# Even layer of a two-block network: a new order of slabs, and latent attention and token shift placed beside other work

## The reference

```python
u = rmsnorm_2(h, norm_mix)
proj = u @ w_in                                   # 1024 x 2208
rw_cols, mla_cols = proj[..., :1792], proj[..., 1792:]
rw_prev = jnp.pad(rw_cols[:, :-1], ((0, 0), (1, 0), (0, 0)))
rw_cols = rw_cols + shift_mu * (rw_prev - rw_cols)          # token shift
y_a = rwkv7_time_mix(...)    # delta rule, 8 heads of 64, group norm, bonus, gate
y_b = mla_attention(...)     # latent attention: norms, q, k, v, rotary, causal softmax, 8 heads
h = h + jnp.concatenate([y_a, y_b], axis=-1) @ w_out
return h + swiglu(rmsnorm_2(h, norm_ffn), ffn_wg, ffn_wu, ffn_wd)
```

## Time and profile before

| | us |
|---|---|
| median of 3 runs (lowest, highest) | 3005.59 (3005.14, 3008.46) |
| the profiled execution's own time | 3002.98 |
| its span, first to last instruction | 3001.2 |
| TensorE, weight loads, VectorE, ScalarE busy | 2737.8, 2273.0, 1806.4, 1453.1 |
| mean granted TensorE clock | 0.941 |
| first split product of the even layer | 1199.8 |
| first transpose of the delta rule | 1301.6 |
| output projection begins, ends | 1555.8, 1583.8 |

### The profile page before, as it was taken

One profiled execution on the slowest core, in us unless ns is written; L12 is line 12 of the kernel. 1 busy time (PEld: TensorE's weight loads), 2 busy tenths in 40 slices (PEclk: granted clock), 3 DMA queues, 4 the chain that ended last, 5 costly groups with the idle time before them and its releaser, 6 DMA issues.

```text
span 3001.2 us, 38726 instructions
## 1 busy us (share of the span) xinstructions
PE 2737.8 (91%) x15370; PEld 2273.0 (76%) x15370; DVE 1806.4 (60%) x1887; ACT 1453.1 (48%) x1609; POOL 29.5 (1%) x40
## 2 busy tenths in 40 slices
PE   6999889999788998857679999889999999999998
PEld 3875368888676898847559997678888888888886
DVE  3224455543544785352344553488888888888887
ACT  3225133332334554311134443367777777777775
POOL 0001000000001000000000000000000000000000
PEclk8999999999898999977689999989999999999999
DMA  7546322222231445300014453179999999999996
GB/s 296 189 188 253 112 84 85 98 96 87 79 146 62 151 160 182 118 1 1 1 52 148 168 181 141 43 279 362 343 346 361 348 361 347 343 362 348 360 347 234
DMA packets 84359, 589.81 MB, mean 197 GB/s; under 512 B 9872, under 2 KB 10000, under 8 KB 19472
## 3 DMA queue, kind: packets, MB, share of 16 engines
q1 hardware_dynamic: 82800, 576.16, 51.7%
q10 hardware_dynamic: 1440, 11.93, 1.0%
HBM read 587.01 MB, written 1.05 MB: 196 GB/s over the span
## 4 chain that ended last, share of the span: by engine, by line
PE 85%; DVE 9%; ACT 4%; issue 1%; DMA 1%; POOL 0%; ACTq 0%; DVEq 0%; SPq 0%; POOLq 0%
PE banks L453 22%; PE banks L454 21%; PE banks L455 21%; PE banks L459 19%; DVE ring_rounded L515 1%; ACT ring_rounded L505 1%; DMA ring<-in_stream 1%; PE banks L2530 1%; DVE rstd L729 1%; ACT scratch L869 1%; DVE activations L1289 1%; PE banks L805 0%; DVE nmax L841 0%; DVE aT L742 0%; DVE aT L1947 0%
## 5 line engine op out<-in xcount | busy, mean ns | idle before, releaser
L515 DVE TENSOR_TENSOR ring_rounded<-ring,ring_rounded 128x2048 fp32r<-128x2048 f32 (+3 forms) x162 | 328.0, 2028 | 460.8 <-ACT ring_rounded L505 459.9
L454 PE MATMUL banks<-ring_rounded,activations_rounded 128*128 128x512 f32 x1344 | 527.5, 392 | 0.0
L454 PE MATMUL banks<-aT_rounded,ring_rounded 128*128 128x256 f32 (+1 forms) x1552 | 501.4, 323 | 0.0
L505 ACT ACTIVATE ring_rounded<-ring 128x2048 fp32r<-128x2048 f32 (+3 forms) x162 | 274.9, 1701 | 396.5 <-PE banks L455 381.1
L453 PE MATMUL banks<-aT_rounded,ring_rounded 128*128 128x256 f32 (+1 forms) x1104 | 332.7, 301 | 20.4 <-DVE aT_rounded L751 11.6
L455 PE MATMUL banks<-aT_rounded,ring_rounded 128*128 128x256 f32 (+1 forms) x1104 | 330.9, 300 | 0.0
L454 PEld LDWEIGHTS banks<-aT_rounded,ring_rounded 128*128 128x128 f32 x1552 | 301.9, 194 | 21.0
L454 PEld LDWEIGHTS banks<-ring_rounded,activations_rounded 128*128 128x128 f32 x1344 | 252.7, 188 | 52.3
L2704 DVE TENSOR_TENSOR ring_rounded<-ring,tables_rounded 128x2048 fp32r<-128x2048 f32 x112 | 253.7, 2287 | 23.3 <-ACT tables_rounded L2622 22.6
L2704 DVE TENSOR_TENSOR ring_rounded<-ring,aT_rounded 128x2048 fp32r<-128x2048 f32 x112 | 254.4, 2286 | 11.6 <-ACT aT_rounded L2622 11.0
L2622 ACT ACTIVATE tables_rounded<-ring 128x2048 fp32r<-128x2048 f32 x112 | 215.0, 1920 | 89.7 <-DMA ring<-in_stream 76.4
(11 more groups left out here) (302 smaller groups left out, 4899.6 us busy)
## 6 DMA issues: line engine op xcount, KB each, us to landing
ring<-in_stream SPq DMA_DIRECT2D x501, 1024.0 KB, 5.4
ring<-in_stream SPq DMA_DIRECT2D x32, 704.0 KB, 5.5
ring<-in_stream SPq DMA_DIRECT2D x28, 768.0 KB, 6.2
activations<-in_rpb ACTq DMA_DIRECT2D x2, 1536.0 KB, 6.5
ring<-in_stream SPq DMA_DIRECT2D x6, 512.0 KB, 5.0
tables<-in_tab_b ACTq DMA_DIRECT2D x1, 2436.0 KB, 8.6
tables<-in_tab_a ACTq DMA_DIRECT2D x1, 2304.0 KB, 8.9
hT<-in_h ACTq DMA_DIRECT2D x1, 2048.0 KB, 15.5
```

Source lines behind the costliest of these rows:

```text
L454: pe.matmul(out, exact(upper), exact(w_lower), start=False, stop=False)
L505: act.activation(exact(upper), w, ACT.Copy).then_inc(g.s["act_pieces"], 1)
L515: dve.tensor_tensor(exact(w), w, rounded(upper), ALU.subtract).then_inc(g.s["dve_pieces"], 1)
```

## The change

It does four things, all in the even layer.

1. Slabs. The 512-column slabs come in the order tiles 12 to 15, the tail, tiles 4 to 7, the lora slab, tiles 0 to 3, tiles 8 to 11. The tail slab is laid out with 224 columns (64 of them zero, so that the shared key lands on partitions 64 to 95) and is split, so its two tiles are split products.
2. even_in_pe, even_in_act and even_in_dve replace the projection, the delta rule's preparation and the latent preparation. Token shift is done per slab (2, 4, 4, 4 tiles), the latent norms and the products of q, k, v and the decay, gate and kk products stand between the slabs. Some passes of VectorE are merged (the factor LN_DECAY moves into ScalarE's exponentials; A~ and R~ are written to their places directly). The delta rule's TensorE program starts when "shifted 11" is there too.
3. delta_pe, delta_act and delta_dve call beside(i) behind levels 0 to 4 (i = 9t + level) and behind the four chunk steps (i = 9t + 5 + step). i = 0, 1: the rotary turns; 2 to 12: rounds 0 to 10 of latent attention; 13: bonus and mean of the first half; 14: its variance; 15: its norm, affine and bonus. The second half's group norm follows behind the delta rule. ScalarE's program has its beside of level 4 ahead of the copies of NV, WT and Z.
4. Buffers: latent q, outputs and probabilities live in places that were free (hT's unused token half, the ring's spare place, mod_rows), and out_pe reads the latent part of its input from there.

The core of the diff; the moved bodies of rope_*, mean_*, variance_* and affine_* are those of before at half width, and attn_pe_step, attn_dve_step, attn_act_step are the loop bodies of before.

```diff
-    cols("w_in_0_2", None, [r(512 * i, 512) for i in range(4)] + [r(2048, 160)])
+    cols("w_in_0_2", None, [r(1536, 512)])
+    out.append(("w_in_0_2", None, KD, [(2048, 224)]))
+    cols("w_in_0_2", None, [r(512, 512)])
     out.append(("lora", None, 0, None))
+    cols("w_in_0_2", None, [r(0, 512), r(1024, 512)])
...
+        if name == "w_in_0_2" and lists[0][0] == 2048:
+            w = np.zeros((D, 224), np.float32)
+            w[:, 0:P], w[:, 192:224] = x[name][:, 2048:2176], x[name][:, 2176:2208]
+            stream[n, :, :224 * KD] = w.reshape(KD, P, 224).transpose(1, 0, 2).reshape(P, -1)
...
+def even_in_pe(g, pe):
     g.x = lambda k: (g.half_upper(k), g.aT[:, k, 0:L])
-    for i in range(4):
-        outs = [(("e", 4 * i + j), slice(0, L), (P * j, P), None, ("mm", "e", 4 * i + j)) for j in range(4)]
-        products(g, pe, g.slabs[g.next_slab], KD, outs, "projection", ("x", "mix0") if i == 0 else None)
+    products(g, pe, g.slabs[g.next_slab], KD, tiles_of(3), "projection", ("x", "mix0"))
+    tail = [(("e", 16), slice(0, L), (0, P), None, ("mm", "e", 16)),
+            (("e", 17), (slice(0, 96), slice(0, L)), (P, 96), None, ("mm", "e", 17))]
+    products(g, pe, g.slabs[g.next_slab], KD, tail, "projection")
+    products(g, pe, g.slabs[g.next_slab], KD, tiles_of(1), "projection")
...
+    pe.wait_ge(g.s["dve_delta"], g.at("shifted", 12))
+    pe.wait_ge(g.s["act_delta"], g.at("tanh w"))
+    for j in range(4):
+        for i, r in enumerate((slice(0, 64), slice(64, 128))):
+            pe.wait_ge(*g.bank_free())
+            ps = g.open(("lora", j, i))
...
+    pe.wait_ge(g.s["act_latent"], g.at("lat sq"))
+    for i, ts in enumerate(((0, 1), (2,))):
         pe.wait_ge(*g.bank_free())
-        ps = g.open(("e", t))
-        out = ps[0:P, 0:L] if m == P else ps[64:96, 0:L]
-        for k in range(KD):
-            a = 160 * k + P * (t - 16)
-            mm(pe, out, w[:, a:a + m], rounded(g.half_upper(k)), k == 0, False)
-            last = mm(pe, out, w[:, a:a + m], rounded(g.aT[:, k, 0:L]), False, k == KD - 1)
-        last.then_inc(g.s["pe_projection"], 1)
-        g.count("pe_projection", ("mm", "e", t))
-    g.also("pe_projection", ("used", n))
-
-
-def even_proj_act(g, act):
-    for t in range(18):
-        if t % 4 == 0 and t < 12:
-            upper_act(g, act, 1)
+        ps = g.open(("lat", i))
...
+    products(g, pe, g.slabs[g.next_slab], KD, tiles_of(0), "projection")
+    pe.wait_ge(g.s["act_delta"], g.at("kk sq"))
+    for i in range(2):
+        pe.wait_ge(*g.bank_free())
+        ps = g.open(("kk", i))
...
+    pe.wait_ge(g.s["dve_latent"], g.at("lat normed"))
+    wuq = w[:, 1024:2560].rearrange("p (k c) -> p k c", k=2)
+    wukv = w[:, 2560:3584].rearrange("p (h w c) -> p h w c", h=8, w=2)
+    for a in range(4):
+        pe.wait_ge(*g.bank_free())
+        ps = g.open(("mla q", a))
...
+    products(g, pe, g.slabs[g.next_slab], KD, tiles_of(2), "projection")
+    for a in range(4):
+        pe.wait_ge(*g.bank_free())
+        ps = g.open(("mla k", a))
...
+    upper_act(g, act, 1)
+    for t in range(12, 16):
+        tile(t)
+    upper_act(g, act, 2)
+    x = g.prj[:, 12:14, 1:257]
+    act.wait_ge(g.s["dve_delta"], g.at("shifted", 12))
...
+        dve.tensor_tensor(g.shift[:, 0:n, :], x[:, :, 0:L], x[:, :, 1:257], ALU.subtract).then_inc(g.s["dve_delta"], 1)
+        g.count("dve_delta")
+        dve.wait_ge(g.s["dve_delta"], g.so_far("dve_delta"))
+        for t in range(n):
+            dve.scalar_tensor_tensor(x[:, t, 1:257], g.shift[:, t, :], g.v("shift_mu_0_2", a + t), x[:, t, 1:257],
+                                     ALU.mult, ALU.add).then_inc(g.s["dve_delta"], 1)
...
+    lower_dve(g, dve, 1)
+    tiles(12, 2)
+    lower_dve(g, dve, 4)
+    tiles(4, 4)
+    lower_dve(g, dve, 1)
...
+    dve.wait_ge(g.s["act_latent"], g.at("lat rms"))
+    dve.reciprocal(g.lat_rms[:, :, :], g.lat_rms[:, :, :]).then_inc(g.s["dve_latent"], 1)
...
+    lower_dve(g, dve, 1)
+    dve.wait_ge(g.s["act_delta"], g.at("sig w", 3))
...
+    lower_dve(g, dve, 1)
+    tiles(0, 4)
+    dve.wait_ge(g.s["act_delta"], g.at("kk norm", 1))
...
+    dve.tensor_tensor(g.bt[:, :, :], g.rw_kk[:, :, :], g.rw_a[:, :, :], ALU.mult).then_inc(g.s["dve_delta"], 1)
+    g.count("dve_delta")
     dve.wait_ge(g.s["act_delta"], g.at("exp before"))
-
-    dve.scalar_tensor_tensor(g.w4[:, :, :], g.rw_kk[:, :, :], -1.0, g.w4b[:, :, :], ALU.mult, ALU.mult).then_inc(g.s["dve_delta"], 1)
-    g.count("dve_delta")
-    dve.wait_ge(g.s["dve_delta"], g.so_far("dve_delta"))
-    dve.tensor_copy(g.ar[:, :, :, 0, :], split(g.w4[:, :, :])).then_inc(g.s["dve_delta"], 1)
+    dve.scalar_tensor_tensor(g.ar[:, :, :, 0, :], split(g.rw_kk[:, :, :]), -1.0, split(g.lnw[:, :, :]),
+                             ALU.mult, ALU.mult).then_inc(g.s["dve_delta"], 1)
...
+    tiles(8, 4)
...
+def beside_delta(g, kind, e, attentions, i):
+    if i < 2:
+        for a in ((0, 1), (2, 3, 4))[i]:
+            {"pe": rope_pe, "act": lambda *_: None, "dve": rope_dve}[kind](g, e, a)
+    elif i < 2 + len(steps_of(attentions)) + 3:
+        if i == 2 and kind == "act":
+            keys_act(g, e)
+        {"pe": attn_pe_step, "act": attn_act_step, "dve": attn_dve_step}[kind](g, e, "mla", attentions, i - 2)
+    elif i == 13:
+        {"pe": bonus_pe, "act": lambda *_: None, "dve": bonus_dve}[kind](g, e)
+        {"pe": mean_pe, "act": mean_act, "dve": mean_dve}[kind](g, e, 0)
+    elif i == 14:
+        {"pe": variance_pe, "act": variance_act, "dve": lambda *_: None}[kind](g, e, 0)
+    elif i == 15:
+        {"pe": lambda *_: None, "act": affine_act, "dve": finish_dve}[kind](g, e, 0)
...
+def bonus_pe(g, pe):
+    pe.wait_ge(g.s["dve_delta"], g.at("rkk", 3))
...
+def finish_dve(g, dve, tt):
+    y, s = of_half(g.y, tt), of_half(g.bt, tt)
+    dve.wait_ge(g.s["act_delta"], g.at("free", ("d var", tt)))
+    dve.reciprocal(s, s).then_inc(g.s["dve_delta"], 1)
...
+                x = g.aT[:, k, 0:T] if attended is None or k < 4 else attended(k - 4)
...
+    only("pe", even_in_pe)
+    only("act", even_in_act)
+    only("dve", even_in_dve)
...
+    beside = lambda i: beside_delta(g, kind, e, mla, i)
     for t in range(2):
-        only("pe", delta_pe, t)
-        only("act", delta_act, t)
-        only("dve", delta_dve, t)
-    only("dve", delta_out_dve)
-    only("act", delta_out_act)
-    only("pe", delta_out_pe)
+        only("pe", delta_pe, t, beside)
+        only("act", delta_act, t, beside)
+        only("dve", delta_dve, t, beside)
+    only("pe", mean_pe, 1)
+    only("dve", mean_dve, 1)
+    only("act", mean_act, 1)
+    only("pe", variance_pe, 1)
+    only("act", variance_act, 1)
+    only("dve", finish_dve, 1)
+    only("act", affine_act, 1)
```

750 lines of the change are left out of this document (369 added, 381 removed).

## The result

The changed kernel takes **2928.59 us** (median of 4 runs, 2924.45 to 2930.19) against 3005.36 (3003.96 to 3008.46, 4 runs of the kernel before beside it): a ratio of 0.9746, 95% interval 0.9733 to 0.9758, 76.8 us less. The forecast was 2933, range 2910 to 2955.

A forecast was written before the change was run, and what follows sets the result against it. Bound by a chain over three engines, not one engine's capacity. 23.2 - 15.1 + 64.8 = 72.9 us gained takes the profiled 3002.98 to 2930; the median lies 2.6 above: 2933 us, range 2910 to 2955.

The forecast's parts named there:

- Part 1: Projection and preparation: from 101.9 to 78.7 us, VectorE ending it, TensorE's floor 74.1; gain 23.2 us.
- Part 1 does not deliver: Rival: a ring of waits in the preparation, which ends at its upper bound 93.6; 2948 us, chance 0.12.
- Part 2: Delta rule with latent steps between: from 173.3 to 188.4 us, net +15.1.
- Copy of the shared key: First latent scores wait for ScalarE's 1.91 us copy of the shared key: +0.9 us.
- Chunk steps: Latent steps behind four chunk steps: +4.0 us at full clock, +10.8 at the lower, taken as +7.
- low clock: Rival: inserted steps do not hold the clock up in the delta rule; +16, 2949 us, chance 0.20.
- Bonus and mean: Last level of the second half: TensorE queues behind VectorE's 1.7 us of products, then 3 x 0.87: +5.0 us.
- 512-column reciprocal and what follows it: Reciprocal (3.36 us), multiply, affine and four adds stand in front of the next chunk's eviction: +4.4 us.
- Latent steps at the levels and banks: Delta rule: steps at levels 3 and 4 +1.0, second half's level 0 +0.8, shared banks +1.0 us.
- Part 3: Way to the output projection: 80.9 us becomes 14.1, output projection +2 from starting at the lower clock; gain 64.8 us.
- High clock: Rival: full clock holds through chunk steps and outputs of the delta rule; -24, 2909 us, chance 0.15.
- Slower: Rival: TensorE waits a step's whole round at 11 places; 3016 us at 8.5 each, 2995 at full clock; chance 0.03.

The follow-up runs named there:

- experiment 4: Changed kernel without the 1024-column reciprocal of the key norm, a constant written in the norm's place: 2929.2 us.
- experiment 7: Changed kernel with ScalarE's preparation reordered: second piece's pass ahead of tanh, sigmoid and latent tiles, latent roots ahead of the key squares: 2922.7 us.
- experiment 3: Changed kernel with the shared key turned first and copied to the heads behind level 1 instead of level 2: 2925.4 us.
- experiment 1: Changed kernel with the eleven latent steps and the shared key's copy run one after the other behind the delta rule's second half: 2945.2 us.
- experiment 5: Changed kernel with the bonus's four VectorE element products moved from i = 13 to i = 8, beside the first output block: 2924.9 us.
- experiment 2: Changed kernel with the first tokens' closing operations moved from behind the second half's second chunk step to behind its last: 2925.1 us.
- Experiment 6: Changed kernel with eight unused 128 x 128 x 512 filler products added to each of the two output blocks: 2938.5 us.
- experiments 9 and 10: On a kernel with late closing operations, split bonus and reordered ScalarE: four latent steps moved into first output block, 2922.6 us; or four fillers per output block, 2927.4 us.

## Why the prediction was right, and which terms were off

**Part 1** was right in size and cause: 78.7 forecast, 78.7 measured, VectorE at the end (experiment 4: without 6.55 us of it the end moves), TensorE's busy time 73.88 for a floor of 74.1. What it did not say is how near the two ends are: VectorE's chain is worth 1.5 us, and the next gain lay in ScalarE's order (2.6 us, experiment 7, of which 1.2 went again before NV), in two waits that the forecast had counted as given, the 2.6 us for pieces and the 3.4 for the root. "Part 1 does not deliver" (93.6) did not come.

**Part 2** was forecast at +15.1 and came at +10.8; halves of 92 and 97 against 93.5 and 90.6. By term:
- Copy of the shared key: +0.9 forecast, a wait of 3.10 seen; removing it gave 0.5 up to NV, less than a half varies by, and nothing over the stretches (experiment 3). The wait was mis-sized; its cost was small, as forecast.
- Chunk steps: +7, between 4.0 and 10.8; measured 9.4 (experiment 1). They ran at the lower level nearly throughout (0.51), so the upper bound was the nearer one. On its first half the rival "low clock" was right.
- Bonus and mean: +5.0. Level 4's end to NV takes 5.0 us in the changed kernel (1417.0 to 1422.04); 2.7 of it was the order of VectorE's products (experiment 5).
- 512-column reciprocal and what follows it, ahead of a chunk's eviction: +4.4; a wait of 6.12 and 5.4 us by its removal (experiment 2). ScalarE's affine and the 0.56 us wait for it had been counted too low.
- Latent steps at the levels and banks: +2.8, less 4 regained from the clock. Experiment 1 gives +0.8 - 2.8 for both, the copy included: about right. The banks' +1.0 can't be told apart in it; the one wait of a step for its banks that a row shows is the 1.67 us of experiment 3, which in the changed kernel lies under the wait for the copy.
- **What failed is the clock in the second half.** The forecast had the clock's help at 4 us in the levels and 2 in the first transposes and none in the chunk steps. Its second half, which it put at 97, came at 90.6, since the chunk steps there began at full clock, 2.9 us that are gone when the levels ahead hold no latent steps (experiment 1). Some 3 us of the rest of the difference I can't put to a term: rotary turns, mean and first transposes were not measured apart.

**Part 3** was right: 14.1 forecast (its terms as listed add up to 13.9), 14.5 measured; the output projection starts at the lower level and takes 1.7 us more, for +2.

**The rule and the trace.** The forecast set the output block's rows (busy all the time at 0.50) against a rule and went by the rows. The changed kernel bears that out: its first half's chunk steps and output block together are 42 us in which TensorE stops for no more than 0.7 us at a time, at 0.51 and 0.50. Experiment 6 shows that the block can run at full clock, experiments 9 and 10 that fewer or other wide products did not bring it there, or only at its end. The Trainium skill, "TensorE: Matmul & The Clock Gate", section "Why this matters for your kernels", would have the clock up in such a stream without idle gaps; the changed kernel's 42 us disagree with it. Only in experiment 7 did the clock come up within such a stream, for some 4 us, and it fell again in an output block without a gap.

**The rivals.** "High clock" (2909) needed full clock in the output blocks: excluded. "Low clock" (2949) came in the first half's chunk steps alone. "Slower" needed 7.5 us at each of eleven places; the steps cost 4.5 us in all by the stretches, 8.4 by the medians. Later stages: nothing beyond the scatter between executions.

Open: why the granted clock comes back for the last chunk step in some kernels (experiment 7), why the same levels run at 0.93 in one kernel and 0.89 in another, and the 2.1 us ahead of the first split product beyond their lying within the scatter. Token shift beside the products and the order of the slabs were not undone one by one; Part 1 rests on its own sum and on experiments 4 and 7.

## What to carry to other kernels

A serial stage placed step by step into the waits of another costs only what sticks out (here 4.5 us for 25 by the stretches, 8.4 by the medians), if each place holds one step, if its inputs are ready, and if no long VectorE instruction stands between two links of a recurrence: put that one where its engine idles for longer than it lasts. Price a wait by what becomes due when it is gone: 6.55 us of reciprocal on the last chain were worth 1.5 there and 0.5 at NV, a wait of 3.10 no more than 0.5, one of 6.12 was worth 5.4. Where single medians scatter as much as the effect, compare stretches between two fixed instructions of the trace, and read from kernels that share a stretch's code how far it repeats.

## What was unexpected of the hardware

- A stream of products without gaps ran at 1.2 GHz for 42 us (1332.20 to 1374.10, clock 0.51 and 0.50), and eight products of 128 x 128 x 512 among those of a block raised it to full clock within it (0.95 from 1360.00 on). Four did only at the first block's very end (0.51 over the block). In the changed kernel itself the sixteen 128 x 128 transposes right behind that stream begin at 1.2 GHz (3.42 us for 1.94 at full clock), and the 48 products behind them run at full clock (5.16 us, as in the first half).
- Work added to a stage made it faster: levels of the second half 50.7 us at 0.87 without latent steps, 47.9 at 0.93 with them (49.2 to 49.4 in three other kernels with the same levels, so by 1.4 us at least).
- An earlier start changed the speed of the same products behind it: with 1.5 or 2.6 us less ahead of them, the first half's products up to NV took 46.2 or 46.3 us and not 45.1.
- The clock carries over: full or half clock at the head of a stretch was worth 1.8 us in the 14.5 us behind the filler blocks, and 1.7 in the output projection, which starts behind 8 us in which TensorE is idle.
